# The halo columns of a causal convolution, computed in buffers of their own

## The chip, the cores and the metric

The kernel runs on the 8 cores of one Trainium2 chip. Each core computes one of the 8 sequences of the batch, with no exchange between cores. The metric is the device time in microseconds (us) of the slowest core. Each core has five engines that run their own queue of instructions in a fixed order and wait for each other through semaphores: TensorE (PE) for matmuls, VectorE (DVE), ScalarE (ACT), GpSimd (POOL), and SyncE (SP), which here only starts DMA transfers.

## The reference

Two layers work on x of 2048 tokens by 1024 features. Layer A is a gated MLP with a spatial mix over 128-token chunks. Layer B, which the change touches, is this:

```python
xb, g = jnp.split(h @ w_in, 2, axis=-1)          # each 1536 wide
xp = jnp.pad(xb, ((0, 0), (3, 0), (0, 0)))
xc = conv_b + conv_w[3] * xp[:, 3:3 + S]
for k in range(3):
    xc = xc + conv_w[k] * xp[:, k:k + S]         # causal, width 4
r = sigmoid(xh @ gate_a_w + gate_a_b)            # xh: xc in 12 heads of 128
i = sigmoid(xh @ gate_x_w + gate_x_b)
log_a = -8 * r * softplus(-lam); a = exp(log_a)
bterm = sqrt(-expm1(2 * log_a)) * (i * xc)
h_t = a_t * h_(t-1) + bterm_t                    # scan over the tokens
x = x + (h_t * silu(g)) @ w_out
```

An RMS norm stands ahead of each layer and one more at the end.

## The kernel before

Both layers walk over 4 blocks of 512 tokens. In layer B features lie on the partitions and tokens along the free axis, so one head (here: a chunk, c = 0 to 11) of one block is a tile of 128x512. A chunk runs through these steps, each named by its line:

- PE makes the branch input into a PSUM bank (L929, 8 matmuls) and the gate input into another (L936, 8 matmuls).
- ACT starts the convolution (L940): XC = w3 * bank + bias.
- DVE adds the three shifted taps k = 2, 1, 0 (L946), on columns 1 to 511, 2 to 511 and 3 to 511. Columns 0 to 2 also need the last three columns of the block before, which are kept in `halo`. After each DVE tap POOL multiplies 1, 2 or 3 halo columns by the tap's weight (L952, into HD) and adds them to the first columns of XC (L956). All of these name the same key for XC, so they follow one another: DVE tap, POOL add, DVE tap, POOL add, DVE tap, POOL add.
- ACT saves the last four columns of the bank as the next block's halo (L959) and casts XC to bf16 (L966, XCB); PE multiplies it by the two gate matrices (L971, L976).
- ACT: tanh of the two gates (L989, L992), exp (L995) and, after POOL has squared the result (L999), a square root (L1009). Tanh and exp are in one activation table and the square root is in another, so each switch between them costs a table load. ACT also makes tanh of the gate path (L979).
- DVE: L982 (gate path, reads PSUM), L1002 (THI and XC), L1012, the scan L1015 and L1021 (the output tile yTB). POOL keeps the scan's last column (L1019).

Working tiles come in rings: XC, THR, A, THI and THG have three buffers, XCB two. A reader of a PSUM bank counts as a writer of it, so the readers of one bank follow in program order; the halo save L959 is the last reader, and PE waits for it before it writes the bank again. An instruction also waits by semaphore for earlier ones of its own engine, except on PE.

The order on each engine is not that of the code. A list scheduler (`_schedule`) simulates the program with its own costs and always takes the ready instruction with the longest path behind it; the queues are then fixed. A change in dependencies so moves instructions everywhere. In each block chunks 0 to 2 form the head; then come three pairs of chunks whose L940 stand side by side on ACT, (4, 5), (7, 8) and (10, 11), with single chunks between them (in the first block the pairing lies elsewhere). From one pair's L940 to the next pair's is called a group: three chunks. In the tail come the output matmuls (L1038), the residual add (L545), the final norm, and the next block's norm and transposes (L523).

## Time and profile before

| | |
|---|---|
| median of 3 runs | 1095.09 us (1093.13 to 1096.6) |
| profiled execution, its own time | 1098.17 us |
| its span, slowest core (core 5) | 1096.6 us (the cores: 1077.4 to 1096.6) |
| PE busy | 857.4 us, 78% |
| DVE busy | 623.3 us, 57% |
| ACT busy | 579.1 us, 53% |
| POOL busy | 288.7 us, 26% |

The profile is one execution on the slowest core. Layer A ends and layer B begins at about 570 us. A matmul's end is modelled, and spans on POOL are rough. All the rows below are of core 5.

### The profile page before, as it was taken

What the parts mean: (1) busy time and instruction counts of PE and PEld (TensorE: products, weight loads), DVE (VectorE), ACT (ScalarE), POOL (GpSimd) and SP (SyncE); (2) the same over time, 40 slices, a digit from 0 to 9 for tenths busy, and PEclk for the clock granted to TensorE, in tenths of its full rate; (3) what the DMA queues carried; (4) which work ended last, traced back from release to release, by engine and by line L of the source; (5) the groups of instructions that cost most, each with busy time, mean ns of one, the idle gap of its engine ahead of it and who ended that gap; (6) DMA issues with size and microseconds to landing.
All of it is one profiled execution on the core that took longest, in us unless ns stands there. A gap on an engine that the chain in (4) does not pass through costs nothing.

```text
span 1096.6 us, 13728 instructions; the slowest of 8 cores (1077.4 to 1096.6 us)
## 1 busy us (share of the span) xinstructions
PE 857.4 (78%) x3884; PEld 398.0 (36%) x3884; DVE 623.3 (57%) x1021; ACT 579.1 (53%) x916; POOL 288.7 (26%) x524
## 2 busy tenths in 40 slices
PE   5697999999999999999462677676675775857576
PEld 4433445444544444444231222332233322332222
DVE  1335643486427743475031678746876578747876
ACT  2556314632236314532131788667866778568873
POOL 1122010211002100100010554325541445314542
PEclk9998999999999999999776788876887878959888
DMA  9999995899449980991928700100001000010001
GB/s 172 214 198 139 159 130 84 120 134 144 66 56 144 141 121 1 152 129 28 88 50 142 116 1 1 77 0 1 0 1 77 0 1 0 20 59 0 1 1 77
DMA packets 83038, 83.53 MB, mean 76 GB/s; under 512 B 20882, under 2 KB 73106, under 8 KB 82963
## 3 DMA queue, kind: packets, MB, share of 16 engines
q0 software_dynamic: 60864, 64.75, 41.9%
q1 hardware_dynamic: 22100, 17.91, 5.8%
q8 instruction: 32, 0.52, 0.2%
q14 instruction: 42, 0.34, 0.1%
HBM read 139.01 MB, written 8.39 MB: 134 GB/s over the span
## 4 chain that ended last, share of the span: by engine, by line
PE 46%; ACT 14%; issue 13%; DVE 11%; DMA 7%; SPq 3%; POOL 3%; DVEq 0%; ACTq 0%; POOLq 0%
PE ps L753 8%; PE ps L759 8%; PE ps L714 8%; PE ps L810 8%; DVE XC L946 3%; PE ps L1038 3%; PE ps L929 3%; DMA winB<-b_w_in 3%; PE ps L523 3%; SPq L857 2%; PE ps L936 2%; DMA x_sb<-x 2%; ACT XC L940 1%; SPq L611 1%; DMA stg<-a_w_in 1%
## 5 line engine op out<-in xcount | busy, mean ns | idle before, releaser
L929 PE MATMUL ps<-hT,winB 128*128 128x512 bf16 x384 | 122.5, 464 | 69.3 <-ACT halo L959 56.6
L946 DVE SCALAR_TENSOR_TENSOR XC<-ps,cw_pp,XC 128x511 f32<-128x511 f32 (+2 forms) x144 | 103.2, 743 | 105.0 <-ACT XC L940 81.6
L759 PE MATMUL ps<-hT,stg 128*128 128x512 bf16 x512 | 136.7, 383 | 2.1 <-DVE SS L778 1.9
L753 PE MATMUL ps<-hT,stg 128*128 128x512 bf16 x512 | 135.3, 379 | 0.1
L936 PE MATMUL ps<-hT,winB 128*128 128x512 bf16 x384 | 98.0, 405 | 38.4 <-DVE THG L982 19.8
L810 PE MATMUL ps<-woutA,yT 128*128 128x512 bf16 x512 | 124.9, 384 | 0.0
L687 POOL DMA_DIRECT2D stg<-a_w_in x48 | 42.7, 891 | 310.9 <-PE ps L714 141.8
L714 PE MATMUL ps<-stg,hT 128*128 128x512 bf16 x512 | 116.2, 385 | 3.0 <-DMA stg<-a_w_in 2.2
L1038 PE MATMUL ps<-woutB,yTB 128*128 128x512 bf16 x384 | 92.2, 397 | 21.3 <-DVE THG L982 18.4
L523 PE MATMUL ps<-ident,xs 128*128 128x128 f32 x256 | 52.3, 344 | 61.9 <-ACT xs L515 34.6
L929 PEld LDWEIGHTS ps<-hT,winB 128*128 128x128 bf16 x384 | 42.6, 114 | 136.4 <-issue 110.3
L494 ACT ACTIVATE xs<-x_sb 128x1024 f32<-128x1024 f32 x48 | 50.5, 1053 | 64.9 <-DVE x_sb L545 49.4
L772 ACT ACTIVATE GU<-ps 128x512 f32<-128x512 f32 x64 | 38.1, 596 | 85.3 <-PE ps L753 56.3
L722 DVE BATCH_NORM_STATS2 stats<-vn 128x6 f32<-128x512 bf16 x64 | 40.5, 683 | 73.3 <-ACT vn L718 73.3
L956 POOL TENSOR_TENSOR XC<-XC,HD 128x1 f32<-128x1 f32 (+2 forms) x144 | 52.9, 368 | 109.4 <-DVE XC L946 103.2
L714 PEld LDWEIGHTS ps<-stg,hT 128*128 128x128 bf16 x512 | 50.2, 99 | 65.3 <-issue 10.4
L533 DVE TENSOR_SCALAR hT<-ps,nw_pp 128x128 bf16<-128x128 f32 x128 | 44.9, 351 | 48.3 <-PE ps L523 37.6
L936 PEld LDWEIGHTS ps<-hT,winB 128*128 128x128 bf16 x384 | 38.5, 102 | 93.3 <-issue 55.4
L952 POOL TENSOR_SCALAR HD<-halo,cw_pp 128x1 f32<-128x1 f32 (+2 forms) x144 | 63.7, 443 | 24.1 <-POOL XC L956 19.6
L810 PEld LDWEIGHTS ps<-woutA,yT 128*128 128x128 bf16 x512 | 50.3, 99 | 51.9 <-issue 1.9
L753 PEld LDWEIGHTS ps<-hT,stg 128*128 128x128 bf16 x512 | 48.9, 98 | 55.3 <-issue 2.9
L523 PEld LDWEIGHTS ps<-ident,xs 128*128 128x128 f32 x256 | 40.8, 178 | 77.5 <-issue 71.8
(85 smaller groups left out, 1355.9 us busy)
## 6 DMA issues: line engine op xcount, KB each, us to landing
stg<-a_w_in POOLq DMA_DIRECT2D x48, 1024.0 KB, 15.7
x_sb<-x SPq DMA_DIRECT2D x4, 2048.0 KB, 14.8
out<-x_sb SPq DMA_DIRECT2D x16, 512.0 KB, 2.7
winB<-b_w_in POOLq DMA_DIRECT2D x2, 2304.0 KB, 26.1
woutA<-a_w_out POOLq DMA_DIRECT2D x4, 1024.0 KB, 21.3
woutB<-b_w_out POOLq DMA_DIRECT2D x2, 1536.0 KB, 16.7
winB<-b_w_in POOLq DMA_DIRECT2D x2, 768.0 KB, 16.3
ws_raw<-a_w_s SPq DMA_DIRECT2D x1, 512.0 KB, 7.6
```

The lines of the kernel that those rows point to most:

```text
L494: P.op("act", lambda e: e.activation(out=junk[:, :], in_=x_sb[:, jt, :], func=AF.Square, accum_out=ss_t[:, jt:jt + 1]), reads=[xkey], writ ...
L523: P.op("pe", lambda e, bank=bank, q=q, dk=dk, xt=xt: e.transpose(out=bank[:, q * 128:(q + 1) * 128], in_=xt[:, dk * 128:(dk + 1) * 128], i ...
L714: P.op("pe", lambda e, bank=bank, stg=stg, dk=dk, j=j, hT=CUR["hT"]: e.matmul(bank[:, :], lhsT=hT[:, dk, j * 128:(j + 1) * 128], rhs=stg[: ...
L753: P.op("pe", lambda e, bU=bU, stU=stU, dk=dk, ci=ci, hT=CUR["hT"]: e.matmul(bU[:, :], lhsT=stU[:, dk, ci * 128:(ci + 1) * 128], rhs=hT[:, ...
L759: P.op("pe", lambda e, bG=bG, stG=stG, dk=dk, ci=ci, hT=CUR["hT"]: e.matmul(bG[:, :], lhsT=stG[:, dk, ci * 128:(ci + 1) * 128], rhs=hT[:, ...
L810: P.op("pe", lambda e, bank=bank, cc=cc, j=j, dh=dh: e.matmul(bank[:, :], lhsT=yT[:, cc, j * 128:(j + 1) * 128], rhs=woutA[:, cc, dh * 512 ...
L929: P.op("pe", lambda e, bX=bX, dk=dk, c=c, hT=CUR["hT"]: e.matmul(bX[:, :], lhsT=winB[:, dk, c * 128:(c + 1) * 128], rhs=hT[:, dk, :], star ...
L936: P.op("pe", lambda e, bG=bG, dk=dk, c=c, hT=CUR["hT"]: e.matmul(bG[:, :], lhsT=winB[:, dk, BW + c * 128:BW + (c + 1) * 128], rhs=hT[:, dk ...
L946: P.op("dve", lambda e, XC=T["XC"], bX=bX, k=k, sh=sh, c=c: e.scalar_tensor_tensor(out=XC[:, sh:512], in0=bX[:, 0:512 - sh], scalar=cw_pp[ ...
L952: P.op("pool", lambda e, hd=hd, k=k, sh=sh, c=c: e.tensor_scalar(out=hd[:, 0:sh], in0=halo[:, c, 4 - sh:4], scalar1=cw_pp[:, k * 12 + c:k ...
L956: P.op("pool", lambda e, hd=hd, XC=T["XC"], sh=sh: e.tensor_tensor(out=XC[:, 0:sh], in0=XC[:, 0:sh], in1=hd[:, 0:sh], op=ALU.add), reads=[ ...
L1038: P.op("pe", lambda e, bank=bank, c=c, j=j, dh=dh: e.matmul(bank[:, :], lhsT=yTB[:, c, j * 128:(j + 1) * 128], rhs=woutB[:, c, dh * 512:(d ...
```

## The change

The columns 0 to 2 get buffers of their own. ACT's L944 (was L940) and the three DVE taps L950 (was L946) now write columns 3 to 511 only, and no POOL instruction stands between them. Beside them POOL copies three halo columns into XH (L957), DVE copies the bank's first three columns behind them (L959, new), and POOL computes the three outputs in HC: w3 and bias (L961), then for each tap a product (L967, HD) and an add (L971). A last POOL copy writes HC into columns 0 to 2 of XC (L974), under a key of its own, kXCh, for which the cast L983 (was L966) and L1019 (was L1002) also wait. HD has two buffers where it had three, XH and HC have two each, and allocations are rounded to 32 bytes where they were rounded to 64. A chunk has 9 small POOL instructions where it had 6, and one more on DVE. Later lines of before move by 17: the halo save is L976, THR L1006, A L1012, the square L1016, the root L1026, the scan L1032.

```diff
@@ -432,7 +432,7 @@
 
     def alloc(name, shape, dt, at=None):
         nbytes = int(np.prod(shape[1:])) * (4 if dt == F32 else 2)
-        nbytes = (nbytes + 63) // 64 * 64
+        nbytes = (nbytes + 31) // 32 * 32
         if at is None:
             off = cur[0]
             cur[0] += nbytes
@@ -843,7 +843,9 @@
                 P.dma("sp", lambda e: e.dma_start(out=NFW[0][:, :],
                                                   in_=norm_f_w_d.partition_broadcast(128)),
                       "nfw", writes=["nfw"])
-            HDr = Ring("HD", [alloc("HD%d" % i, [128, 4], F32)[0] for i in range(3)])
+            HDr = Ring("HD", [alloc("HD%d" % i, [128, 4], F32)[0] for i in range(2)])
+            XHr = Ring("XH", [alloc("XH%d" % i, [128, 6], F32)[0] for i in range(2)])
+            HCr = Ring("HC", [alloc("HC%d" % i, [128, 4], F32)[0] for i in range(2)])
             XCr = Ring("XC", [alloc("XC%d" % i, [128, 512], F32)[0] for i in range(NSET)])
             XCBr = Ring("XCB", [alloc("XCB%d" % i, [128, 512], BF16)[0] for i in range(2)])
             THRr = Ring("THR", [alloc("THR%d" % i, [128, 512], F32)[0] for i in range(NSET)])
@@ -937,35 +939,50 @@
                             bG[:, :], lhsT=winB[:, dk, BW + c * 128:BW + (c + 1) * 128],
                             rhs=hT[:, dk, :], start=(dk == 0), stop=(dk == 7)),
                             reads=CUR["hk"] + [("winB", 1, hf)], writes=[bkG])
+                    kXCh = ("XCh",) + tuple(T["kXC"][1:])
+                    T["kXCh"] = kXCh
                     P.op("act", lambda e, XC=T["XC"], bX=bX, c=c: e.activation(
-                        out=XC[:, :], in_=bX[:, :], func=AF.Identity,
+                        out=XC[:, 3:512], in_=bX[:, 3:512], func=AF.Identity,
                         scale=cw_pp[:, 36 + c:37 + c], bias=cb_pp[:, c:c + 1]),
                         reads=[bkX, "cw", "cb"], writes=[T["kXC"]])
                     for k in (2, 1, 0):
                         sh = 3 - k
                         P.op("dve", lambda e, XC=T["XC"], bX=bX, k=k, sh=sh, c=c: e.scalar_tensor_tensor(
-                            out=XC[:, sh:512], in0=bX[:, 0:512 - sh],
-                            scalar=cw_pp[:, k * 12 + c:k * 12 + c + 1], in1=XC[:, sh:512],
+                            out=XC[:, 3:512], in0=bX[:, 3 - sh:512 - sh],
+                            scalar=cw_pp[:, k * 12 + c:k * 12 + c + 1], in1=XC[:, 3:512],
                             op0=ALU.mult, op1=ALU.add),
                             reads=[bkX, T["kXC"], "cw"], writes=[T["kXC"]])
+                    XH, kXH = XHr.next()
+                    HC, kHC = HCr.next()
+                    P.op("pool", lambda e, XH=XH, c=c: e.tensor_copy(out=XH[:, 0:3], in_=halo[:, c, 1:4]),
+                         reads=[("halo", c)], writes=[kXH])
+                    P.op("dve", lambda e, XH=XH, bX=bX: e.tensor_copy(out=XH[:, 3:6], in_=bX[:, 0:3]),
+                         reads=[bkX], writes=[kXH])
+                    P.op("pool", lambda e, HC=HC, XH=XH, c=c: e.tensor_scalar(
+                        out=HC[:, 0:3], in0=XH[:, 3:6], scalar1=cw_pp[:, 36 + c:37 + c],
+                        scalar2=cb_pp[:, c:c + 1], op0=ALU.mult, op1=ALU.add),
+                        reads=[kXH, "cw", "cb"], writes=[kHC])
+                    for k in (2, 1, 0):
                         hd, khd = HDr.next()
-                        P.op("pool", lambda e, hd=hd, k=k, sh=sh, c=c: e.tensor_scalar(
-                            out=hd[:, 0:sh], in0=halo[:, c, 4 - sh:4],
+                        P.op("pool", lambda e, hd=hd, XH=XH, k=k, c=c: e.tensor_scalar(
+                            out=hd[:, 0:3], in0=XH[:, k:k + 3],
                             scalar1=cw_pp[:, k * 12 + c:k * 12 + c + 1], scalar2=None, op0=ALU.mult),
-                            reads=[("halo", c), "cw"], writes=[khd])
-                        P.op("pool", lambda e, hd=hd, XC=T["XC"], sh=sh: e.tensor_tensor(
-                            out=XC[:, 0:sh], in0=XC[:, 0:sh], in1=hd[:, 0:sh], op=ALU.add),
-                            reads=[khd, T["kXC"]], writes=[T["kXC"]])
+                            reads=[kXH, "cw"], writes=[khd])
+                        P.op("pool", lambda e, hd=hd, HC=HC: e.tensor_tensor(
+                            out=HC[:, 0:3], in0=HC[:, 0:3], in1=hd[:, 0:3], op=ALU.add),
+                            reads=[khd, kHC], writes=[kHC])
+                    P.op("pool", lambda e, HC=HC, XC=T["XC"]: e.tensor_copy(out=XC[:, 0:3], in_=HC[:, 0:3]),
+                         reads=[kHC], writes=[kXCh])
                     P.op("act", lambda e, bX=bX, c=c: e.activation(
                         out=halo[:, c, :], in_=bX[:, 508:512], func=AF.Copy),
                         reads=[bkX], writes=[("halo", c)])
                     if os.environ.get("KCAST", "act") == "pool":
                         P.op("pool", lambda e, XCB=T["XCB"], XC=T["XC"]: e.tensor_copy(out=XCB[:, :], in_=XC[:, :]),
-                             reads=[T["kXC"]], writes=[T["kXCB"]])
+                             reads=[T["kXC"], kXCh], writes=[T["kXCB"]])
                     else:
                         P.op("act", lambda e, XCB=T["XCB"], XC=T["XC"]: e.activation(
                             out=XCB[:, :], in_=XC[:, :], func=AF.Copy),
-                            reads=[T["kXC"]], writes=[T["kXCB"]])
+                            reads=[T["kXC"], kXCh], writes=[T["kXCB"]])
                     bR, bkR = PS.next()
                     T["bR"], T["bkR"] = bR, bkR
                     P.op("pe", lambda e, bR=bR, XCB=T["XCB"], c=c: e.matmul(
@@ -1002,7 +1019,7 @@
                     P.op("dve", lambda e, THI=T["THI"], XC=T["XC"]: e.scalar_tensor_tensor(
                         out=THI[:, :], in0=THI[:, :], scalar=1.0, in1=XC[:, :],
                         op0=ALU.add, op1=ALU.mult),
-                        reads=[T["kTHI"], T["kXC"]], writes=[T["kTHI"]])
+                        reads=[T["kTHI"], T["kXC"], T["kXCh"]], writes=[T["kTHI"]])
 
                 def st3(T):
                     c = T["c"]
@@ -1015,7 +1032,7 @@
                     P.op("dve", lambda e, Ht=T["XC"], At=T["A"], THI=T["THI"], c=c: e.tensor_tensor_scan(
                         out=Ht[:, :], data0=At[:, :], data1=THI[:, :], initial=hstate[:, c:c + 1],
                         op0=ALU.mult, op1=ALU.add),
-                        reads=[T["kA"], T["kTHI"], ("hstate", c)], writes=[T["kXC"]])
+                        reads=[T["kA"], T["kTHI"], ("hstate", c)], writes=[T["kXC"], T["kXCh"]])
                     P.op("pool", lambda e, Ht=T["XC"], c=c: e.tensor_copy(out=hstate[:, c:c + 1], in_=Ht[:, 511:512]),
                          reads=[T["kXC"]], writes=[("hstate", c)])
                     P.op("dve", lambda e, THG=T["THG"], Ht=T["XC"], c=c: e.scalar_tensor_tensor(
```

The scheduler sets the queues anew. First POOL, in the third block, around the pair of chunks 7 and 8 (XC1 and XC2). Before, the six small instructions of each chunk alternate:

```order
L956 TENSOR_TENSOR XC1_100<-XC1_100,HD0_96 128x1
L952 TENSOR_SCALAR HD0_96<-halo_87,cw_pp_81 128x1
L956 TENSOR_TENSOR XC2_101<-XC2_101,HD0_96 128x1
L952 TENSOR_SCALAR HD0_96<-halo_87,cw_pp_81 128x1
L956 TENSOR_TENSOR XC1_100<-XC1_100,HD1_97 128x2
L952 TENSOR_SCALAR HD1_97<-halo_87,cw_pp_81 128x2
L956 TENSOR_TENSOR XC2_101<-XC2_101,HD1_97 128x2
L952 TENSOR_SCALAR HD1_97<-halo_87,cw_pp_81 128x2
L956 TENSOR_TENSOR XC1_100<-XC1_100,HD2_98 128x3
L952 TENSOR_SCALAR HD2_98<-halo_87,cw_pp_81 128x3
L956 TENSOR_TENSOR XC2_101<-XC2_101,HD2_98 128x3
L952 TENSOR_SCALAR HD2_98<-halo_87,cw_pp_81 128x3
```

Now, from the first product of chunk 7's chain to its copy into XC (HC1 and XH1 belong to chunk 7, HC0 and XH0 to chunk 8; six more instructions for chunk 8 follow, the last its own copy):

```order
L961 TENSOR_SCALAR HC1_101<-XH1_99,cw_pp_81,cb_pp_82 128x3
L967 TENSOR_SCALAR HD1_97<-XH1_99,cw_pp_81 128x3
L967 TENSOR_SCALAR HD0_96<-XH1_99,cw_pp_81 128x3
L971 TENSOR_TENSOR HC1_101<-HC1_101,HD1_97 128x3
L971 TENSOR_TENSOR HC1_101<-HC1_101,HD0_96 128x3
L967 TENSOR_SCALAR HD1_97<-XH1_99,cw_pp_81 128x3
L961 TENSOR_SCALAR HC0_100<-XH0_98,cw_pp_81,cb_pp_82 128x3
L967 TENSOR_SCALAR HD0_96<-XH0_98,cw_pp_81 128x3
L971 TENSOR_TENSOR HC1_101<-HC1_101,HD1_97 128x3
L974 COPY XC1_103<-HC1_101 128x3
```

Ten instructions stand from L961 to L974 for the first chunk of the pair, two of which are the second chunk's, and all come after DVE's copy L959.

Second ACT, at the same pair. Before, with a halo save ahead of each cast (L966):

```order
L940 ACTIVATE XC1_100<-ps4,cb_pp_82,cw_pp_81 128x512
L940 ACTIVATE XC2_101<-ps0,cb_pp_82,cw_pp_81 128x512
L992 ACTIVATE THI0_110<-ps3,bx_pp_84 128x512
L979 ACTIVATE THG1_114<-ps5 128x512
L979 ACTIVATE THG2_115<-ps1 128x512
L1009 ACTIVATE THR0_104<-THR0_104,quarter_89 128x512
L959 ACTIVATE halo_87<-ps4 128x4
L966 ACTIVATE XCB1_103<-XC1_100 128x512
L959 ACTIVATE halo_87<-ps0 128x4
L966 ACTIVATE XCB0_102<-XC2_101 128x512
```

Now both halo saves stand ahead of both casts (L983), the next chunk's start L944 comes right behind them (XC0), and products and adds of POOL have to be through before the casts:

```order
L944 ACTIVATE XC1_103<-ps4,cb_pp_82,cw_pp_81 128x509
L944 ACTIVATE XC2_104<-ps0,cb_pp_82,cw_pp_81 128x509
L1012 ACTIVATE A0_110<-THR0_107,k1_pp_85 128x512
L1009 ACTIVATE THI0_113<-ps3,bx_pp_84 128x512
L996 ACTIVATE THG1_117<-ps5 128x512
L996 ACTIVATE THG2_118<-ps1 128x512
L1026 ACTIVATE THR0_107<-THR0_107,quarter_89 128x512
L976 ACTIVATE halo_87<-ps4 128x4
L976 ACTIVATE halo_87<-ps0 128x4
L983 ACTIVATE XCB1_106<-XC1_103 128x512
L983 ACTIVATE XCB0_105<-XC2_104 128x512
```

Third POOL again, where the chunk between two pairs has its turn (chunk 6, XC0). Before, the squares of the pair (L999) and then the adds:

```order
L999 TENSOR_TENSOR THR1_105<-A1_108 128x512
L999 TENSOR_TENSOR THR2_106<-A2_109 128x512
L956 TENSOR_TENSOR XC0_99<-XC0_99,HD0_96 128x1
L952 TENSOR_SCALAR HD0_96<-halo_87,cw_pp_81 128x1
L956 TENSOR_TENSOR XC0_99<-XC0_99,HD1_97 128x2
L952 TENSOR_SCALAR HD1_97<-halo_87,cw_pp_81 128x2
L956 TENSOR_TENSOR XC0_99<-XC0_99,HD2_98 128x3
L952 TENSOR_SCALAR HD2_98<-halo_87,cw_pp_81 128x3
L1019 COPY hstate_88<-XC1_100 128x1
```

Now the pair's squares (L1016) and then the whole chain of chunk 6, eight instructions:

```order
L1016 TENSOR_TENSOR THR1_108<-A1_111 128x512
L1016 TENSOR_TENSOR THR2_109<-A2_112 128x512
L961 TENSOR_SCALAR HC0_100<-XH0_98,cw_pp_81,cb_pp_82 128x3
L967 TENSOR_SCALAR HD0_96<-XH0_98,cw_pp_81 128x3
L971 TENSOR_TENSOR HC0_100<-HC0_100,HD0_96 128x3
L967 TENSOR_SCALAR HD1_97<-XH0_98,cw_pp_81 128x3
L967 TENSOR_SCALAR HD0_96<-XH0_98,cw_pp_81 128x3
L971 TENSOR_TENSOR HC0_100<-HC0_100,HD1_97 128x3
L971 TENSOR_TENSOR HC0_100<-HC0_100,HD0_96 128x3
L974 COPY XC0_102<-HC0_100 128x3
```

The squares keep their place; the chain behind them is longer by two instructions, and starts only once DVE's copy L959 has ended.

## Rows read from the trace of the kernel before

**Rows 1.** Windows: us; busy time and instructions per engine; TensorE clock; DMA share; GB/s.
```profile
40.00:560.00 520.00, 482.56 (x2425) 230.17 (x2426) 261.30 (x485) 200.54 (x328) 64.12 (x89) 0.96 0.80 115
...
600.00:1096.00 496.00, 336.71 (x1304) 143.06 (x1304) 344.70 (x501) 360.27 (x558) 213.69 (x407) 0.81 0.08 24
```

**Rows 2.** Waits after 600 us: waiter, what it waited for; total us, times, longest.
```profile
DVE XC L946 <- POOL XC L956: 22.7, 15, 17.5
ACT halo L959 <- DVE XC L946: 22.5, 10, 20.5
ACT XCB L966 <- POOL XC L956: 22.1, 36, 1.5
```

**Rows 3.** Timeline of ACT, one group: start, duration, instruction, [idle before <-releaser].
```profile
777.53 1.43 ACT L940 ACTIVATE XC<-ps,cb_pp,cw_pp 128x512 f32<-128x512 f32 x2
...
782.98 0.63 ACT L966 ACTIVATE XCB<-XC 128x512 bf16<-128x512 f32 x1 [0.33 <-POOL XC L956]
784.01 0.17 ACT L959 ACTIVATE halo<-ps 128x4 f32<-128x4 f32 x1 [0.40 <-POOL HD L952]
785.25 0.63 ACT L966 ACTIVATE XCB<-XC 128x512 bf16<-128x512 f32 x1 [1.06 <-POOL XC L956]
...
795.54 0.63 ACT L966 ACTIVATE XCB<-XC 128x512 bf16<-128x512 f32 x1 [0.47 <-POOL XC L956]
...
799.62 1.44 ACT L940 ACTIVATE XC<-ps,cb_pp,cw_pp 128x512 f32<-128x512 f32 x2
```

**Rows 4.** Timeline of DVE in the same group.
```profile
778.40 2.07 DVE L946 SCALAR_TENSOR_TENSOR XC<-ps,cw_pp,XC 128x511 f32<-128x511 f32 x3 [0.88 <-ACT XC L940]
...
780.99 2.19 DVE L946 SCALAR_TENSOR_TENSOR XC<-ps,cw_pp,XC 128x510 f32<-128x510 f32 x3
783.09 0.69 DVE L1012 TENSOR_TENSOR THI<-THI,THR 128x512 f32<-128x512 f32 x1
783.89 1.28 DVE L1015 TENSOR_TENSOR_SCAN XC<-A,hstate,THI 128x512 f32<-128x512 f32 x1
785.28 0.69 DVE L1021 SCALAR_TENSOR_TENSOR yTB<-XC,THG 128x512 bf16<-128x512 f32 x1
785.89 1.28 DVE L982 SCALAR_TENSOR_TENSOR THG<-THG,ps 128x512 f32<-128x512 f32 x2
```

**Rows 5.** Timeline of POOL in the same group.
```profile
783.06 0.80 POOL L952 TENSOR_SCALAR HD<-halo,cw_pp 128x3 f32<-128x3 f32 x1 [0.17 <-POOL XC L956]
784.08 1.08 POOL L956 TENSOR_TENSOR XC<-XC,HD 128x3 f32<-128x3 f32 x1 [0.21 <-POOL HD L952]
785.33 0.81 POOL L952 TENSOR_SCALAR HD<-halo,cw_pp 128x3 f32<-128x3 f32 x1 [0.17 <-DVE XC L1015]
```

**Rows 6.** Lines L952 and L956: minimum, median and maximum ns.
```profile
L952 POOL TENSOR_SCALAR HD<-halo,cw_pp x144: 282/306/1266, 566.4 to 1063.5; 128x1 f32<-128x1 f32 x48, 128x2 f32<-128x2 f32 x48, 128x3 f32<-128x3 f32 x48
...
L956 POOL TENSOR_TENSOR XC<-XC,HD x144: 186/193/1085, 574.3 to 1064.5; 128x1 f32<-128x1 f32 x48, 128x2 f32<-128x2 f32 x48, 128x3 f32<-128x3 f32 x48
```

**Rows 7.** Groups by form: busy us, mean ns; idle before.
```profile
L497 DVE TENSOR_SCALAR ms_t<-ss_t 128x1 f32<-128x1 f32 x28 | 3.8, 148 | 4.1 <-ACT xs L494 4.1
```

**Rows 8.** Windows: the group between two pairs of L940.
```profile
777.53:799.62 22.09, 13.53 (x54) 5.44 (x54) 17.61 (x24) 18.08 (x28) 12.64 (x24) 0.85 0.00 0
```

**Rows 9.** Timeline of ACT: after the last pair of a block.
```profile
800.95 0.82 ACT L995 ACTIVATE A<-THR,k_pp 128x512 f32<-128x512 f32 x1
801.65 0.69 ACT L992 ACTIVATE THI<-ps,bx_pp 128x512 f32<-128x512 f32 x1
...
808.24 0.63 ACT L966 ACTIVATE XCB<-XC 128x512 bf16<-128x512 f32 x1 [1.06 <-POOL XC L956]
810.11 1.28 ACT L989 ACT_TABLE_LOAD   x1 [1.23 <-PE ps L971]
```

**Rows 10.** Timelines of POOL, then PE, in the first block of layer B.
```profile
600.74 0.90 POOL L886 DMA_DIRECT2D woutB<-b_w_out  x1 [23.04 <-DMA winB<-b_w_in]
...
600.35 5.93 PE L936 MATMUL ps<-hT,winB 128*128 128x512 bf16 x16 [18.63 <-DMA winB<-b_w_in]
...
607.19 0.38 PE L971 MATMUL ps<-XCB,waB 128*128 128x512 bf16 x1
```


## The prediction

> **What bounds the kernel now.** I read the busy time by stage first, then the waits of layer B, then the timelines of one group of three chunks. After 600 us no engine is full over the whole stage: ACT is busy for 360.27 of 496 us, DVE for 344.70, PE for 336.71, POOL for 213.69 [rows 1]. The change touches only what comes after. Within a group, however, ACT is busy for 18.08 of 22.09 us [rows 8], and since its queue is in fixed order, any wait in it moves all that follows. So layer B is bound by ACT's queue plus the waits inside it. The waits that this change is about are small in sum: DVE taps for POOL adds 22.7 us, 17.5 of it once; ACT's casts for POOL adds 22.1 us in 36 waits; the halo save for DVE 22.5 us, 20.5 once [rows 2]. In a group the reader sees them as idle times of 0.33, 0.40, 1.06 and 0.47 us before L966 and L959 [rows 3].
>
> **What the change removes.** Three POOL adds no longer stand between the three DVE taps. In a pair of chunks this was already covered, because DVE alternates between the two: six taps and one L1002 run from 778.40 to 783.18 without a gap [rows 4]. Taking 777.53, the start of the pair's L940, as zero, the last tap ends at 5.65. After the change the taps can't end much earlier, for they start when ACT has made XC. The taps keep their length (509 columns instead of up to 511), the rounding of buffers moves addresses only, and the table loads stay as many, since the switches between square root and tanh in ACT's new queue are 64 as before: I cost these at nothing.
>
> **What it adds on DVE and POOL.** Per chunk one DVE copy of three columns; the nearest row, a tiny L497, takes 148 ns [rows 7]. On POOL a product takes 306 ns in the median and at least 282, an add 193 and at least 186 [rows 6]. A copy I take as an add. Where a small POOL instruction uses the result of the one before, there is a gap, 0.17 behind an add and 0.21 behind a product [rows 5]. The trace of before does not show the chain itself, so it gets a bound from either side.
>
> **The pair, step by step.** DVE's two copies end at 5.65 + 0.30 = 5.95; with a semaphore (0.15, of the size of the gaps in [rows 5]) POOL starts L961 at 6.1. Ten POOL instructions lead to the first chunk's L974: four L967 and two L961 (a product with a bias), 6 x 0.30; three adds and a copy, 4 x 0.19; three gaps of 0.17; together 3.07. Six more lead to the second's: 2 x 0.30, three adds and a copy, 4 x 0.19, and gaps of 0.17, 0.21, 0.17 and 0.17, together 2.08. That gives L974 of the second chunk at 11.25, its cast at 11.4, ended at 12.0. This is the lower bound of a pair.
>
> It holds only if POOL runs undisturbed, and the rows speak against that. The product at 783.06 took 0.80 us in place of 0.30, and beside it DVE ran L1012 (783.09, 0.69); the add at 784.08 took 1.08 in place of 0.19, until DVE's scan L1015 ended (783.89 + 1.28 = 785.17); the product at 785.33 took 0.81 beside L1021 (785.28, 0.69) [rows 4, 5]. While DVE runs L1002, L1012, L1015 or L1021, one small POOL instruction gets through for each, and it ends when DVE's does. Beside the taps L946 nothing is stretched. In the new order the copies L959 are followed on DVE by the gate path's product (L999, half of the 1.28 of two L982), L1012, L1015 and L1021. So POOL gets two instructions done by 6.7, then one each beside L1012, the scan and L1021, until 7.4, 8.75 and 9.5, and the other five of ten (0.17 + 3 x 0.30 + 0.19 + 0.17 + 0.18 = 1.6) by 11.1. With 2.08 more, L974 of the second chunk ends at 13.2, its cast runs from 13.35 to 14.0. I take this one, since the nearest rows stand in the same group beside the same DVE instructions.
>
> The Trainium skill, "SBUF — State Buffer", section "Who interferes with whom", says that a DVE instruction with two SBUF inputs and a GpSimd instruction that reads SBUF exclude each other for a whole instruction, while one with at most one SBUF input leaves GpSimd alone. The rows agree, 1.08 us beside the scan. By that rule the pair's cast ends at 14.0, without it at 12.0.
>
> Before, the second cast of the pair ends at 785.88, so 8.35 [rows 3]. ACT can do nothing else in between: both casts stand ahead of the next L944 in its queue. The three pairs of a block come to: 14.0 - 8.35 = 5.6 for the first; 4.2 for the second, where ACT's L1012 and L1009 (before L995 and L992, from 800.95 to 802.34, some 1.4 us [rows 9]) now stand behind the pair's L944 and fill part of the wait; for the third, where before they stood there (cast ended at 808.87, 9.25 after its L940 at 799.62) and now don't, 14.0 - 9.25 + 1.4 = 6.1, less 1.2 for the wait for PE that follows before and is then covered [rows 3, 9] = 4.9. Together 14.7 (lower bound 3.6 + 2.2 + 2.9 = 8.7).
>
> **The single chunk between pairs.** In the first of a block's groups POOL has the pair's two squares ahead of the whole chain. The chain then runs while DVE is in L1012, L1012 and two scans, and its last three instructions end with these: the cast comes about 2.3 us late where before it waited 0.47 [rows 3]. That is 1.8 a block. In the next group most of the chain stands ahead of the squares, and I take nothing; in the last no chunk follows. Bounds 0 and 3 x 1.8 = 5.4.
>
> **The head of a block.** Chunks 0 to 2 have no full ACT queue around them. Each cast waits for a chain of 8 POOL instructions (some 3.1 us) where there were three adds between taps. Between nothing and one pair's delay (5.6) I take 2.5.
>
> **The first block** is different. Before, POOL stands in its queue before the DMA issue L886 until 600.74, and the taps of chunks 0 and 1 with it [rows 10]; this holds the 17.5 and 20.5 us above [rows 2]. In the new order L888 comes behind the chains of the first three chunks, so their convolution is done during that wait. The gate matmuls can't use it: PE's queue now has 19 matmuls on winB ahead of the first, where 16 and 5 stood before it, and the weights arrive at 600.35, so the first gate matmul stays at about 607 [rows 10]. What is left is that the casts and tap chains of chunks 1 and 2 no longer come behind it: -3 in place of +2.5 (bounds 0 and -6).
>
> **Sum.** 14.7 + 1.8 + 2.5 = 19.0 a block, 76 for four, less 5.5 for the first = 70.5. The profiled execution took 1098.17 us with a span of 1096.6, so 1168.7; it stood 3.1 above the median of 1095.09, and the median to expect is 1166. For this case alone the range is 1145 to 1190.
>
> **Rivals.**
> - POOL is not held up (chance 0.20): 8.7 a block and nothing else, 35, less 6 in the first: +29, 1124. For it: spans on POOL are rough, and DVE's long instructions may fall elsewhere once the group has grown. Against it: every group shows the stretched ones.
> - POOL is held up at each single chunk and at each head too (0.13): 14.7 + 5.4 + 5.6 = 25.7 a block, +100 with first block, 1195. For it: in each group DVE's excluding instructions last some 3 x 3.3 = 10 us of 22 and POOL's work grows from 18 to 27 small ones.
> - Faster (0.07): the three columns are ready in time, and the waits for them go. This needs L974 of the second chunk before ACT reaches its cast, at about 6.5 after the pair's start, instead of 11.25. Then each group saves 0.33 + 0.40 + 1.06 + 0.47 = 2.3 us, 12 groups 27, the first block 3: 1065. It decides if DVE's copy L959 stood ahead of the taps; in the new queue it stands behind them, as a reader of the same bank. Against it also: even without any exclusion ten and six instructions need 5.1 us.
> - The order matters little (0.03): delays of casts are taken up in waits for PE (1.23 us at 810.11) and in the tail; the time stays.
>
> My forecast has the remaining 0.57. A difference of 0.3%, about 3 us, is what a measurement of this kernel can tell from none. Faster 0.07, the same 0.03, slower 0.90. The range reaches over the first rival to the second: 1115 to 1200.
>
> **What would show it.** Right: L974's cast wait takes the first place in ACT's waits, 3 to 5 us before the pair's first cast and 1 to 2 before the second; a group of some 27 us; ACT busy as long as before; small POOL instructions of 0.7 to 1.1 us beside L1029, L1032 and L1038; layer A unchanged. Wrong: casts that wait under 1 us, a group of 22 us, or a delay in another place, such as PE waiting for the casts with ACT idle.

## The result: 5.9% slower, and the profile after

The changed kernel takes 1159.31 us (median of 9 runs) where the kernel before takes 1096.3 (10 runs): a ratio of 1.0588, 95% interval [1.057, 1.0605]; the one slow execution of each (1241.18 and 1175.67 us) is left out of the ratio. The range 1115 to 1200 holds it, and the forecast of 1166 was 7 us too high. The profiled execution took 1160.47 us with a span of 1158.9 (core 2; cores 1148.4 to 1158.9).

The first view is the page's busy time, the second the windows of layer A, of layer B and of one group; the columns of the second are those of [rows 1].

```profile
PE 856.0 (74%) x3809; PEld 395.5 (34%) x3884; DVE 633.0 (55%) x1069; ACT 577.0 (50%) x916; POOL 319.2 (28%) x668
```

```profile
40.00:560.00 520.00, 480.36 (x2391) 232.03 (x2440) 261.97 (x486) 202.26 (x331) 64.34 (x89) 0.96 0.81 114
600.00:1158.00 558.00, 335.48 (x1261) 139.80 (x1284) 350.26 (x541) 356.18 (x553) 239.39 (x529) 0.80 0.08 21
799.66:826.65 26.99, 14.05 (x53) 5.28 (x54) 18.99 (x27) 20.09 (x31) 14.18 (x34) 0.86 0.00 1
```

Layer A is as before, and after 600 us 62 us more pass with ACT busy for 356 us where it was busy for 360 [rows 1]. The added time is idle time. The group of three chunks takes 26.99 us where it took 22.09 [rows 8]. The waits after 600 us, to be held against [rows 2], say for what:

```profile
POOL HC L961 <- DVE XH L959: 140.8, 33, 18.5
...
ACT XCB L983 <- POOL XC L974: 100.6, 36, 5.4
...
DVE THI L1019 <- ACT THI L1009: 76.3, 18, 24.9
```

The first row costs nothing by itself: POOL sits idle until there is a chain to do. The second is the forecast's: ACT's casts waited 22.1 us for POOL and now wait 100.6, in as many waits. The third follows from it in part, since THI is made from a gate matmul behind the cast; 24.9 of its 76.3 us are one wait in the first block, and before, the same wait came to 20.4 in all. ACT in the second block, to be held against [rows 3] (a group from one pair's L944 to the next, then the start of another):

```profile
771.23 1.43 ACT L944 ACTIVATE XC<-ps,cb_pp,cw_pp 128x509 f32<-128x509 f32 x2
...
781.33 0.63 ACT L983 ACTIVATE XCB<-XC 128x512 bf16<-128x512 f32 x1 [3.90 <-POOL XC L974]
782.86 0.63 ACT L983 ACTIVATE XCB<-XC 128x512 bf16<-128x512 f32 x1 [0.90 <-POOL XC L974]
...
796.55 0.63 ACT L983 ACTIVATE XCB<-XC 128x512 bf16<-128x512 f32 x1 [5.30 <-POOL XC L974]
...
799.66 1.44 ACT L944 ACTIVATE XC<-ps,cb_pp,cw_pp 128x509 f32<-128x509 f32 x2
...
809.97 0.63 ACT L983 ACTIVATE XCB<-XC 128x512 bf16<-128x512 f32 x1 [4.26 <-POOL XC L974]
811.52 0.63 ACT L983 ACTIVATE XCB<-XC 128x512 bf16<-128x512 f32 x1 [0.92 <-POOL XC L974]
```

The second cast of the pair ends 12.26 and 12.49 after its L944. POOL, and DVE beside it, in two stretches: the single chunk's chain from 790.35, the pair's from 805.43.

```profile
790.35 0.34 POOL L961 TENSOR_SCALAR HC<-XH,cw_pp,cb_pp 128x3 f32<-128x3 f32 x1 [2.26 <-DVE XH L959]
790.67 0.82 POOL L967 TENSOR_SCALAR HD<-XH,cw_pp 128x3 f32<-128x3 f32 x1
791.63 0.42 POOL L971 TENSOR_TENSOR HC<-HC,HD 128x3 f32<-128x3 f32 x1
792.04 3.60 POOL L967 TENSOR_SCALAR HD<-XH,cw_pp 128x3 f32<-128x3 f32 x2
...
805.75 1.10 POOL L967 TENSOR_SCALAR HD<-XH,cw_pp 128x3 f32<-128x3 f32 x2
806.83 1.25 POOL L971 TENSOR_TENSOR HC<-HC,HD 128x3 f32<-128x3 f32 x2
```

```profile
790.71 1.29 DVE L1029 TENSOR_TENSOR THI<-THI,THR 128x512 f32<-128x512 f32 x2
791.92 2.45 DVE L1032 TENSOR_TENSOR_SCAN XC<-A,hstate,THI 128x512 f32<-128x512 f32 x2
794.29 1.27 DVE L1038 SCALAR_TENSOR_TENSOR yTB<-XC,THG 128x512 bf16<-128x512 f32 x2
...
806.00 0.68 DVE L1029 TENSOR_TENSOR THI<-THI,THR 128x512 f32<-128x512 f32 x1
806.79 1.30 DVE L1032 TENSOR_TENSOR_SCAN XC<-A,hstate,THI 128x512 f32<-128x512 f32 x1
```

A product on three columns takes 0.30 us when alone. From 792.04 to 795.64 POOL gets only two done, while DVE runs two scans and two L1038 back to back: one of the two took 1.26 us and the other 2.36, until the second L1038 had ended. Small as they are, these instructions set the time of ACT.

Where the time went, block by block of layer B, from the start of a block's first L931 (L929) to that of the next; the last block ends with the span:

| block | before | after | more | forecast |
|---|---|---|---|---|
| 1 | 150.8 | 168.2 | 17.4 | 13.5 |
| 2 | 130.1 | 145.2 | 15.1 | 19.0 |
| 3 | 128.1 | 144.8 | 16.7 | 19.0 |
| 4 | 117.7 | 133.5 | 15.9 | 19.0 |

Together 65.1. The first L931 comes 2.8 us earlier than L929 did (567.11 for 569.88), so the span is 62.3 longer. A block starts here with its first recorded matmul; in a few blocks the record of the first one is missing and the start is 0.4 us late, as in the second block after (its weight loads begin at 734.87, 0.4 before the first matmul on record).

### The profile page after: what moved, and what is told of

The parts are those of the page before. It is cut to its first block, busy times and chain, and to the rows that moved or that the text cites. A ratio compares the mean times of both kernels' runs of the same rounds, so it can differ in the third digit from the quotient of the medians.

```text
span 1158.9 us, 13784 instructions; the slowest of 8 cores (1148.4 to 1158.9 us)
## 1 busy us (share of the span) xinstructions
PE 856.0 (74%) x3809; PEld 395.5 (34%) x3884; DVE 633.0 (55%) x1069; ACT 577.0 (50%) x916; POOL 319.2 (28%) x668
## 4 chain that ended last, share of the span: by engine, by line
PE 38%; issue 19%; ACT 11%; DVE 11%; DMA 10%; POOL 7%; SPq 2%; DVEq 1%; ACTq 0%; POOLq 0%
PE ps L714 8%; PE ps L810 7%; PE ps L759 7%; PE ps L753 7%; DMA stg<-a_w_in 5%; DVE XC L950 4%; DMA winB<-b_w_in 3%; PE ps L1055 2%; PE ps L523 2%; POOL HC L971 2%; POOL HD L967 2%; ACT THI L1009 2%; SPq L859 2%; PE ps L931 2%; DVE THI L1019 1%
## 5 line engine op out<-in xcount | busy, mean ns | idle before, releaser
L931 PE MATMUL ps<-hT,winB 128*128 128x512 bf16 x375 | 122.5, 472 | 71.9 <-ACT halo L976 52.0
L950 DVE SCALAR_TENSOR_TENSOR XC<-ps,cw_pp,XC 128x509 f32<-128x509 f32 x144 | 102.3, 741 | 96.9 <-ACT XC L944 90.7
L938 PE MATMUL ps<-hT,winB 128*128 128x512 bf16 x376 | 100.5, 408 | 54.5 <-DVE THG L999 43.9
L759 PE MATMUL ps<-hT,stg 128*128 128x512 bf16 x497 | 134.4, 383 | 4.8 <-DVE SS L778 2.7
L753 PE MATMUL ps<-hT,stg 128*128 128x512 bf16 x501 | 132.8, 379 | 0.4
L687 POOL DMA_DIRECT2D stg<-a_w_in x48 | 42.8, 892 | 315.8 <-PE ps L714 144.5
L810 PE MATMUL ps<-woutA,yT 128*128 128x512 bf16 x499 | 122.3, 381 | 0.7
L714 PE MATMUL ps<-stg,hT 128*128 128x512 bf16 x502 | 113.6, 381 | 2.7 <-DMA stg<-a_w_in 1.1
L931 PEld LDWEIGHTS ps<-hT,winB 128*128 128x128 bf16 x384 | 43.3, 116 | 141.7 <-issue 118.5
L1019 DVE SCALAR_TENSOR_TENSOR THI<-THI,XC 128x512 f32<-128x512 f32 x48 | 46.0, 983 | 76.3 <-ACT THI L1009 76.3
L983 ACT ACTIVATE XCB<-XC 128x512 bf16<-128x512 f32 x48 | 29.6, 627 | 100.6 <-POOL XC L974 100.6
L1016 POOL TENSOR_TENSOR THR<-A 128x512 f32<-128x512 f32 x48 | 51.8, 1087 | 90.5 <-ACT A L1012 90.5
L967 POOL TENSOR_SCALAR HD<-XH,cw_pp 128x3 f32<-128x3 f32 x144 | 72.2, 509 | 0.3 <-POOL HC L971 0.3
```

The costliest lines, as they stand in the source:

```text
L714: P.op("pe", lambda e, bank=bank, stg=stg, dk=dk, j=j, hT=CUR["hT"]: e.matmul(bank[:, :], lhsT=hT[:, dk, j * 128:(j + 1) * 128], rhs=stg[: ...
L753: P.op("pe", lambda e, bU=bU, stU=stU, dk=dk, ci=ci, hT=CUR["hT"]: e.matmul(bU[:, :], lhsT=stU[:, dk, ci * 128:(ci + 1) * 128], rhs=hT[:, ...
L759: P.op("pe", lambda e, bG=bG, stG=stG, dk=dk, ci=ci, hT=CUR["hT"]: e.matmul(bG[:, :], lhsT=stG[:, dk, ci * 128:(ci + 1) * 128], rhs=hT[:, ...
L810: P.op("pe", lambda e, bank=bank, cc=cc, j=j, dh=dh: e.matmul(bank[:, :], lhsT=yT[:, cc, j * 128:(j + 1) * 128], rhs=woutA[:, cc, dh * 512 ...
L931: P.op("pe", lambda e, bX=bX, dk=dk, c=c, hT=CUR["hT"]: e.matmul(bX[:, :], lhsT=winB[:, dk, c * 128:(c + 1) * 128], rhs=hT[:, dk, :], star ...
L938: P.op("pe", lambda e, bG=bG, dk=dk, c=c, hT=CUR["hT"]: e.matmul(bG[:, :], lhsT=winB[:, dk, BW + c * 128:BW + (c + 1) * 128], rhs=hT[:, dk ...
```

## The experiments

Theories: (A) the chain of small POOL instructions behind the last tap makes the casts late, stretched where DVE runs instructions with two SBUF inputs; (B) it is the new order of the queues; (C) it is the amount of POOL's and DVE's work; (D) it is the new addresses. Each ratio below is to the kernel before, run in the same round. One execution of each kernel was profiled, and the lengths of blocks are from it. They repeat well: in e1, which is as fast as the kernel before, the blocks are 151.2, 129.9, 128.1 and 117.7.

**e1_round32** is the kernel before with the new rounding alone.

```diff
-        nbytes = (nbytes + 63) // 64 * 64
+        nbytes = (nbytes + 31) // 32 * 32
```

> The kernel before with the allocations rounded to 32 bytes instead of 64, and nothing else. Every theory here (the POOL chain, the new queues) expects the time of before within its noise, ratio 0.997 to 1.003. Only if addresses themselves matter would it move, and then part of the 5.9% of the change would be theirs.

1098.29 us, 0.9986 [0.9969, 1.0003]: no part of the loss, as expected. (D) falls, as far as rounding moves addresses.

**e2_cut_chain** keeps the change's queues as scheduled, but then drops the three products and three adds of each chunk from POOL's, so the halo taps are left out.

```diff
+        for e in ENGS:
+            order[e] = [i for i in order[e] if ops[i].tbl != "kill"]
...
-                        P.op("pool", lambda e, hd=hd, XH=XH, k=k, c=c: e.tensor_scalar(
+                        KO = P.op("pool", lambda e, hd=hd, XH=XH, k=k, c=c: e.tensor_scalar(
...
+                        KO.tbl = "kill"
```

> The changed kernel with its queues kept as they are, instruction by instruction, but without the six instructions L967 and L971 of each chunk, so the taps of the halo columns are not computed. The chain from DVE's copy to the cast has then 2 POOL instructions where it had 8. If the length of the chain is the cause, the casts of a pair wait 0.5 us where they wait 5.4, and the time comes back to about that of before: ratio 0.99 to 1.01. If the rival is right, that the queues which the scheduler built anew are the worse ones whatever POOL does, the time stays near that of the change: ratio 1.04 to 1.06.

1115.85 us, 1.0147 [1.0115, 1.0178], between the two expectations (0.99 to 1.01 and 1.04 to 1.06) and much nearer the first. Of 5.9 points of loss 4.4 are the six instructions; the blocks shrink from 168.2, 145.2, 144.8 and 133.5 to 157.8, 133.1, 133.0 and 120.9, so by 10.4, 12.1, 11.8 and 12.6 us. The 1.5 points that stay are the queues' and those of L957, L959, L961 and L974, which still run; no run parts the two. One place where they stand, in ACT and then in PE (L1005 is the cast here, L1010 the gate matmul, L1077 the output matmul):

```profile
814.77 0.63 ACT L1005 ACTIVATE XCB<-XC 128x512 bf16<-128x512 f32 x1 [0.46 <-POOL XC L996]
818.58 1.28 ACT L1028 ACT_TABLE_LOAD   x1 [3.17 <-PE ps L1010]
```

```profile
812.49 5.71 PE L1077 MATMUL ps<-woutB,yTB 128*128 128x512 bf16 x13 [8.90 <-ACT halo L998]
817.99 0.51 PE L1010 MATMUL ps<-XCB,waB 128*128 128x512 bf16 x1
```

The cast is ready early, but thirteen output matmuls stand ahead of the gate matmul in PE's queue.

**e3_memsets** keeps queues, waits and instruction count, and turns the eight instructions of the chain (L961 to L974) into memsets, which read nothing; columns 0 to 2 of XC come out as zeros.

```diff
                         P.op("pool", lambda e, hd=hd, HC=HC: e.tensor_tensor(
                             out=HC[:, 0:3], in0=HC[:, 0:3], in1=hd[:, 0:3], op=ALU.add),
-                            reads=[khd, kHC], writes=[kHC])
+                            reads=[khd, kHC], writes=[kHC]).fn = (
+                                lambda e, HC=HC: e.memset(HC[:, 0:3], 0.0))
```

> The changed kernel, queues and waits kept, but each of the 8 POOL instructions of a chunk's chain from DVE's copy on is a memset of the same output, which reads nothing (columns 0 to 2 of XC are zero). It tells apart why the chain is slow. If DVE's instructions with two SBUF inputs hold up only a POOL instruction that reads SBUF, no memset is stretched beside the scan, the pair's second cast starts some 2 to 3 us after the copy, and the ratio is 1.00 to 1.03. If any POOL instruction is held up beside DVE's work, memsets of 0.5 to 1.2 us stand beside the scan and L1038 and the ratio stays at 1.04 to 1.06.

1114.36 us, 1.0139 [1.0112, 1.0165], as if the chain were gone and within the range of the first expectation. First POOL's groups by form (busy us, mean ns, idle before), then its timeline and DVE's:

```profile
L976 POOL MEMSET HC<- 128x3 f32 x144 | 14.4, 100 | 10.5 <-POOL HC L976 1.1 <-POOL HD L972 0.3
L972 POOL MEMSET HD<- 128x3 f32 x144 | 13.4, 100 | 3.1 <-POOL HD L972 0.3 <-issue 0.2
L957 POOL COPY XH<-halo 128x3 f32<-128x3 f32 x48 | 12.5, 275 | 0.1
```

```profile
811.63 0.10 POOL L976 MEMSET HC<- 128x3 f32 x1
811.66 0.10 POOL L979 MEMSET XC<- 128x3 f32 x1
811.85 0.10 POOL L976 MEMSET HC<- 128x3 f32 x1
812.07 0.10 POOL L979 MEMSET XC<- 128x3 f32 x1
```

```profile
811.64 1.28 DVE L1036 TENSOR_TENSOR_SCAN XC<-A,hstate,THI 128x512 f32<-128x512 f32 x1
```

Four memsets end within 0.54 us beside a scan, and all of the chain's take 100 ns in the mean; the copy L957, which reads SBUF, still averages 275. This bears out the rule of the Trainium skill, "SBUF — State Buffer", section "Who interferes with whom": it is GpSimd's read of SBUF that DVE's second SBUF input excludes, and a GpSimd instruction that only writes is left alone. The run doesn't split the gain between shorter instructions (0.10 for 0.30) and their not being stretched.

**e4_early_copy** is the change with the two copies into XH ahead of the taps, so that the chain can run beside these.

```diff
+                    XH, kXH = XHr.next()
+                    HC, kHC = HCr.next()
+                    P.op("pool", lambda e, XH=XH, c=c: e.tensor_copy(out=XH[:, 0:3], in_=halo[:, c, 1:4]),
+                         reads=[("halo", c)], writes=[kXH])
+                    P.op("dve", lambda e, XH=XH, bX=bX: e.tensor_copy(out=XH[:, 3:6], in_=bX[:, 0:3]),
+                         reads=[bkX], writes=[kXH])
                     for k in (2, 1, 0):
                         sh = 3 - k
...
-                    XH, kXH = XHr.next()
...
```

> The changed kernel with the two copies into XH placed in the program ahead of the three DVE taps, so that POOL's chain runs beside the taps; the scheduler orders the queues anew, and all is computed. If the place of the chain behind the taps is the cause, the chain is mostly over when the taps are, casts wait about 1 us, and the ratio is 0.98 to 1.01. If the amount of POOL work (9 small instructions a chunk instead of 6) is the cause, wherever it stands, the ratio stays above 1.03.

1094.58 us, 0.9961 [0.9944, 0.9978]: two copies moved turn a loss of 5.9% into a gain of 0.4%, with the same instructions (in new queues). The casts of a pair and of the single chunk behind it on ACT, and the two L974 of the pair on POOL:

```profile
781.97 1.24 ACT L983 ACTIVATE XCB<-XC 128x512 bf16<-128x512 f32 x2 [0.57 <-POOL XC L974]
...
793.31 0.62 ACT L983 ACTIVATE XCB<-XC 128x512 bf16<-128x512 f32 x1
```

```profile
777.58 0.34 POOL L961 TENSOR_SCALAR HC<-XH,cw_pp,cb_pp 128x3 f32<-128x3 f32 x1
...
781.69 0.19 POOL L974 COPY XC<-HC 128x3 f32<-128x3 f32 x1
...
782.21 0.18 POOL L974 COPY XC<-HC 128x3 f32<-128x3 f32 x1
```

The chain now begins 1.26 us after the pair's L944 (776.32) and ends 6.07 after it, where the change's ends 11.54 and 11.77 after it. POOL's small instructions are as many, so (C) falls. The queues are new here too, so e4 alone can't tell the chain's place from (B); e2 and e3, which keep the change's queues, put 4.4 to 4.5 of the 5.9 points on the chain, and with them e4 says that it is its place. The casts don't wait less than before: 13.0 us for L974, 6.0 for the copy L950 and 2.7 for the taps, 21.7 together, against 22.1.

**e5_dve_halo** is the kernel before with the halo columns on DVE: three small scalar_tensor_tensor (L951), nothing on POOL.

```diff
-                        P.op("pool", lambda e, hd=hd, k=k, sh=sh, c=c: e.tensor_scalar(
...
+                        P.op("dve", lambda e, XC=T["XC"], k=k, sh=sh, c=c: e.scalar_tensor_tensor(
+                            out=XC[:, 0:sh], in0=halo[:, c, 4 - sh:4],
+                            scalar=cw_pp[:, k * 12 + c:k * 12 + c + 1], in1=XC[:, 0:sh],
+                            op0=ALU.mult, op1=ALU.add),
```

> The kernel before with the halo columns on DVE: behind each tap, one scalar_tensor_tensor of 1, 2 or 3 columns (halo times weight, plus XC) in place of POOL's product and add. No POOL instruction stands between L940 and the cast, and none is held up there. DVE gets 3 small instructions a chunk, 0.15 to 0.25 us each. If what the halo columns cost is POOL's chain with its semaphores and its exclusion beside DVE, ratio 0.97 to 0.99. If DVE's work is the bound of layer B (17.6 of 22.1 us in a group are busy), the added 36 to 50 instructions a block slow it: ratio 1.00 to 1.02.

1109.85 us, 1.0122 [1.0103, 1.0141]: slower, where I had expected a gain; the rival held. DVE from the pair's first tap on, and what ACT makes of it:

```profile
792.29 0.73 DVE L946 SCALAR_TENSOR_TENSOR XC<-ps,cw_pp,XC 128x511 f32<-128x511 f32 x1
793.14 0.22 DVE L951 SCALAR_TENSOR_TENSOR XC<-halo,cw_pp,XC 128x1 f32<-128x1 f32 x1
793.46 1.41 DVE L946 SCALAR_TENSOR_TENSOR XC<-ps,cw_pp,XC 128x510 f32<-128x510 f32 x2
...
797.92 0.41 DVE L951 SCALAR_TENSOR_TENSOR XC<-halo,cw_pp,XC 128x3 f32<-128x3 f32 x2
```

```profile
798.23 1.15 ACT L963 ACTIVATE XCB<-XC 128x512 bf16<-128x512 f32 x2 [2.97 <-DVE XC L951]
```

The pair's taps take 6.04 us where before they took 4.78 with an L1002 among them [rows 4], since each small one costs 0.21 us and a gap of 0.1 on either side; and both casts wait for the last. Work taken off an idle engine was put onto the path.

**e6_halo_sums** takes the halo part out of the chunk altogether: POOL sums the halo's contribution to the next block right after the halo is saved, and DVE adds it in one instruction (the rounding is the new one).

```diff
+                    P.op("dve", lambda e, XC=T["XC"], c=c: e.tensor_tensor(
+                        out=XC[:, 0:3], in0=XC[:, 0:3], in1=hsum[:, c, 0:3], op=ALU.add),
+                        reads=[("hsum", c), T["kXC"]], writes=[T["kXC"]])
...
+                    if tb < NTB - 1:
+                        P.op("pool", lambda e, c=c: e.tensor_scalar(
+                            out=hsum[:, c, 0:3], in0=halo[:, c, 1:4],
...
```

> The kernel before with the halo's part of columns 0 to 2 summed by POOL right after the halo is saved, a whole block ahead (5 small POOL instructions a chunk, on nobody's path), and one DVE add of 3 columns behind the taps. If only what stands behind the taps counts, this is at least as good as the halo taps on DVE: ratio 0.965 to 0.985. If POOL's small instructions cost wherever they stand, because they and DVE exclude each other, it is at 0.99 to 1.01.

1092.97 us, 0.9973 [0.9959, 0.9986]: not the 0.965 to 0.985 of the first expectation but within the other (0.99 to 1.01), though the run doesn't show the reason given there. The casts' waits for the convolution fall to 8.5 us in 13 waits on DVE, from 22.1 in 36, and yet 0.3% is all. In the profiled execution, which was the fastest of its runs, the first block gains 11.6 us (139.2 for 150.8) and the later three lose 4.6 together (130.4, 129.8 and 120.3, for 130.1, 128.1 and 117.7). Taking the halo work from between the taps gained nothing in a steady block. The new queues have waits of their own: ACT's start of the convolution (L942) now waits 13.3 us for POOL's copy of the scan's last column (L1031), where before these waits came to 2.4. What the halo work is worth with the queues kept was not run.

**e7_costed** is the change with small POOL instructions costed in the scheduler nearer to what they take (0.55 us for 0.16 to 0.21).

```diff
+        if o.eng == "pool" and n <= 8:
+            return 0.55
```

> The changed kernel, with one number of the scheduler changed: it takes 0.55 us for a POOL instruction of up to 8 columns, in place of about 0.2, which is nearer to what the trace shows. The program is the same, the queues differ. If the chain has to stand there and no order hides it, ratio 1.03 to 1.055. If the queues, built for a chain of 1.6 us, were most of the loss, ratio 1.00 to 1.02.

1142.13 us, 1.0416 [1.0394, 1.0438]: 1.7 of the 5.9 points come back. The waits:

```profile
PE ps L990 <- ACT XCB L985: 46.1, 18, 3.4
...
ACT XC L946 <- POOL XC L976: 16.9, 6, 2.8
...
ACT XCB L985 <- POOL XC L976: 12.0, 4, 3.1
```

ACT's casts hardly wait for the chain any more, for its queue now has other work there, and still most of the loss stays. Part of the wait has moved to ACT's start of the convolution, L946, which waits 36.5 us for POOL (16.9 for the chain's last copy, 11.3 for the halo copy L959, 8.3 for the copy of the scan's last column, L1038), and PE's waits for casts are 46.1 us, where they were 33.0 in the changed kernel and 6.2 before. As I read it the chain's length is the cause and the order decides who waits for it, though only e2, e3 and e4 test that.

**e8_wout_free** is the kernel before without the tie that makes woutB's load (L886) wait for the winB chunks. It turns to the first block, where the forecast was furthest off.

```diff
-                    ("woutB", q2), reads=[("bch", 2, i) for i in range(2)], writes=[("woutB", q2)])
+                    ("woutB", q2), writes=[("woutB", q2)])
```

> The kernel before, with the two woutB loads L886 issued without their wait for the winB loads, so POOL does not stand in its queue until 600 us and the first taps are not held. It prices by itself what the change does in the first block. If the casts of the first chunks were what the first block waited for, it gains 3 to 6 us: ratio 0.994 to 0.997. If the weights and PE's queue are, it gains nothing, or loses as woutB's 3 MB share the DMA engines with winB: ratio 0.998 to 1.008.

1076.54 us, 0.9824 [0.9798, 0.985]: far more than either expectation (0.994 at best). The first block takes 131.7 us in place of 150.8; the next two stay within 2 us of theirs (128.6, 129.7). PE in that block:

```profile
575.47 0.38 PE L971 MATMUL ps<-XCB,waB 128*128 128x512 bf16 x1 [0.37 <-ACT XCB L966]
...
583.11 2.72 PE L929 MATMUL ps<-hT,winB 128*128 128x512 bf16 x6 [3.80 <-DMA winB<-b_w_in]
```

The first gate matmul runs at 575.47, where before it ran at 607.19 [rows 10]. Either POOL's queue is free now or PE's order is better: the edit did both.

**e12_no_hold** tells these apart: the kernel before with its queues as they were, and only woutB's wait for winB taken away after scheduling.

```diff
+            if o.name == "wfree":
+                o.deps = set(d for d in o.deps if not (
+                    ops[d].is_dma and isinstance(ops[d].sem_key, tuple) and ops[d].sem_key[0] == "winB"))
```

> The kernel before with its queues kept, instruction by instruction, and only the wait of the two woutB loads for winB taken away once the queues are set. It splits the 19 us that the freed loads gained. If POOL's stand in its queue held the first block, ratio 0.980 to 0.986. If it is PE's queue, where 16 gate-path matmuls on the late part of winB stand ahead of all else, the gain is at most the 2 or 3 us of casts: ratio 0.997 to 1.002.

1098.05 us, 1.0024 [1.001, 1.0037]: nothing gained. First POOL, then PE:

```profile
583.95 0.90 POOL L890 DMA_DIRECT2D woutB<-b_w_out  x1
```

```profile
601.00 5.89 PE L940 MATMUL ps<-hT,winB 128*128 128x512 bf16 x16 [21.00 <-DMA winB<-b_w_in]
...
607.81 0.38 PE L975 MATMUL ps<-XCB,waB 128*128 128x512 bf16 x1
```

POOL has issued both loads by 584.85 instead of waiting until 600.74, and the taps of chunks 0 and 1 are done by 586; but 16 gate-path matmuls that need the late weights stand first in PE's queue. Freeing POOL is not enough while PE keeps this order. That the order alone would do is not shown: in e8 the gate matmul of 575.47 needs taps that POOL's wait would have held, so its gain probably needs both.

**e11_after_wout** makes e8's edit in the changed kernel (the same line, no other).

> The change, with the woutB loads issued without their wait. In the first block PE has, in the change, 19 matmuls on winB ahead of the first gate matmul, and some of them need the part that arrives at 600 us. If the late part of the weights and the chain make up the first block (+17 us), the loads change little: ratio 1.050 to 1.060. If the queues come out as in the kernel before with freed loads, it gains about 19 us: ratio 1.038 to 1.045.

1133.68 us, 1.0351 [1.0328, 1.0374], a little more than the better expectation (1.038). The first block drops from 168.2 to 142.5 us; the others stay at 144.4 and 144.5. Here too the first gate matmul comes early (576.87, for 603.47). So the two effects are largely separate: with the loads freed in both kernels the change still loses 10.8 us in the first block (142.5 for e8's 131.7) and 15 to 16 in the next two, where with the loads tied it loses 17.4 in the first. The early convolution that the change brings there was of no use to PE's queue.

**e9_sums_wout** is e6 with e8's edit.

> The halo sums prepared a block ahead, and the woutB loads issued without their wait. The scheduler orders the queues anew. Halo sums alone had its first block at 139.2 us where before has 150.8, and the freed loads alone 131.7. If the two gains in the first block are the same one (no wait of the first taps), the ratio is that of the freed loads, 0.980 to 0.985. If they add up, 0.970 to 0.978.

1087.74 us, 0.993 [0.9911, 0.995]: the gains of 0.27% and 1.76% don't add up, and neither expectation (0.985 at the most) held. The blocks take 133.3, 131.9 and 132.9, so each later block is 2 to 5 us longer than before. Which instruction costs this I did not settle.

**e10_early_wout** is e4 with e8's edit.

> The change with the copies into XH ahead of the taps, and the woutB loads issued without their wait. Early copy alone stood at 0.996 with its first block as before (151.1 us) and the others 2 us shorter. If the first block gains as in the kernel before (19 us), ratio 0.976 to 0.982; if its queues put the gate path of later chunks first, as the change does, 0.990 to 0.996.

1072.09 us, 0.9781 [0.9759, 0.9803]: this beats both kernels and lies in the first expectation. The blocks take 132.2, 125.5 and 130.1. Whether it also beats e8 (0.9824 [0.9798, 0.985]) is open, since the two intervals overlap and the runs were not in the same round.

## Why the prediction was right, and where not

- **The mechanism** held: casts wait for L974, ACT's busy time stays, the group is 27 us, layer A unchanged. PE's waits for the casts grew as well, from 6.2 to 33.0 us. e2 and e3 show the chain's size with the queues kept, and e4 its place.
- **The pair's second cast**: forecast 14.0 after its L944, measured 12.26 and 12.49, though POOL was held up. The first chunk's L974 ended at 10.2 (forecast 11.1), and the second's 1.55 behind it (forecast 2.08; POOL interleaves the two chains, and few gaps are left). The lower bound of 12.0 was nearer, but not for the reason that the rival gave.
- **Groups of the second block**: start to first pair 34.59 before and 35.95 after (+1.4, forecast +2.5); first to second pair 22.24 and 28.43 (+6.2, forecast 5.6 + 1.8 less the 1.4 moved = 6.0); second to third 22.09 and 26.99 (+4.9, forecast 4.2 + 1.4 = 5.6); the rest 51.2 and 53.9 (+2.7, forecast 4.9). The tail takes up part of the last delay, which I named only in the fourth rival. The 1.4 us moved was misread: before, L992 already stood behind the second pair's L940 (778.85), so only L995's 0.7 moved there, and L992's 0.7 moved ahead of the first pair.
- **The single chunk**: between the pairs one is late a block, as forecast, but its cast waited 5.30 us and not about 2.3, because the chain met two L1029, two scans and two L1038, and two of its products got through where I had counted one for each DVE instruction. The next group's single waited 0.55, as forecast nearly nothing. The cast of the single chunk ahead of the first pair, which my working doesn't name, waited 4.22 us too (it started at 766.73; 0.48 before).
- **That the groups came out near is in part luck**: in the first group the pair was delayed by 3.9 us (12.26 for 8.35) and not by 5.6, and the single's cast by 4.8 (5.30 for 0.47) and not by 1.8. The two misses cancel, together with a table load of 1.28 us that now falls into the pair's wait (at 775.20, where before it stood behind the pair's casts at 763.66).
- **The first block**: this step failed. I gave -3 in place of +2.5, and wrote that the gate matmul would stay at about 607; it came at 603.47, 36.4 us after the block's start where it was 37.3 [rows 10], so 0.9 of 3 came. The block then lost 18.3, more than any other. By e2, 10.4 of its 17.4 are the chain and 7.0 the order with the four instructions that e2 keeps.
- **The order of queues**: I costed it only through named moves. It holds up to 1.5 of 5.9 points (e2, e3), so the sum came out near for a partly wrong reason: the chain was sized at 19 a block and is worth 12, and the order, with what e2 keeps of the chain, brought 3 to 7 more.
- **"It decides if DVE's copy stood ahead of the taps"**, the point named for the faster rival, is what e4 did; the gain was 0.4%, not the 3% of that rival. The waits did not go: the casts of e4 still wait 21.7 us. Nor is it sure that they were worth their sum, since in e6 they fell to 8.5 for a gain of 0.3%.

## What to carry to other kernels

A piece of work moved into buffers of its own is off the path only if its result is ready when the consumer is: find the last instruction that its first step waits for, count the chain from there, and look at what the engines beside it run meanwhile. Small GpSimd instructions that read SBUF should stand beside DVE instructions with one SBUF input (here the taps, whose other input is in PSUM), not beside scans and products of two SBUF tiles. And before a wait is removed, look at which queue stands behind it: e12 took POOL's wait of 23.0 us [rows 10] away for nothing, and e8, which had a new order as well, gained 20 us.

## What the runs showed of the hardware that I had not expected

Beside back-to-back DVE instructions with two SBUF inputs a small POOL instruction doesn't always get its turn between them: two products took 3.60 us beside two scans and two L1038, the longer of them 2.36. A memset of three columns is untouched by a scan and takes 0.10 us, against 0.30 for a product. A DVE scalar_tensor_tensor on one to three columns takes 0.21 us with 0.1 us of gap around it, so six of them in a pair cost 1.9 us.
